# Retention heads: squares kept as a high and a low part, summed by two matmuls in the middle of the next unit

## The chip, the cores and the metric

One core of one Trainium2 chip runs one program. The metric is the device time of one execution in microseconds (us); lower is better. The engines are TensorE (PE), VectorE (DVE), ScalarE (ACT), GpSimd (POOL) and the DMA queues. Each engine works through its own list of instructions in order, and engines meet only at semaphores.

## The reference

Two transformer blocks follow each other on 512 tokens of width 1024. The change touches the retention branch of the second block's mixer: 8 heads, keys of 64, values of 128. Cut to what matters:

```python
def _retention(q, k, v, gn_gain):
    inner = jnp.einsum('bhncd,bhnkd->bhnck', qc, kc) * decay
    ...
    o = (o_inner + o_cross).reshape(B, H, S, dv)
    mu = jnp.mean(o, axis=-1, keepdims=True)
    var = jnp.mean(jnp.square(o - mu), axis=-1, keepdims=True)
    on = (o - mu) * lax.rsqrt(var + GN_EPS) * gn_gain
    return on...

r_out = jax.nn.silu(g_r) * _retention(...)
gate_a, gate_r = jnp.split(jax.nn.sigmoid(g_merge), 2, axis=-1)
mixed = gate_a * (a_out @ w_branch_nsa) + gate_r * (r_out @ w_branch_ret)
```

Everything is kept transposed: the 128 features of a head lie on the partitions and the 512 tokens along the row. So the variance of a token is a sum over partitions, which the kernel takes as a matmul with a 128x128 matrix of ones. The values are centred beforehand, so `o - mu` is what the value matmuls give.

## The kernel before

Nearly all products are done in three matmuls (`mm3`, lines 177 to 179): an operand is split into a high part that the fast type (fp32r) holds, made by ACT as a copy, and a low part, the difference, made by DVE or POOL; then high by high, high by low and low by high are added in one PSUM bank. A sum of squares is done otherwise: one matmul on plain fp32 data, `ones` by `gn_sq`.

Weights come in chunks of 128x1024 from DRAM into two raw buffers `w_raw`. ACT makes `w_hi` (line 146), DVE makes `w_lo` (line 151), and when that is done SP issues the load of the chunk after next (line 2652). Conversion runs two chunks ahead of PE.

The retention stage has 8 units, one for each head `h`. It follows the attention of the same mixer, and its queue orders are written out by hand. In unit `h`:

- PE (`pe_part`, line 2329): `score(h+1)`, then `squares_summed(h-1)` (line 2346), then the first four tiles of `fill(h)` (a 1024-wide product that makes one tile of the merge gates, 24 matmuls in all), `values(h)` (12 matmuls), then the other four tiles of `fill(h)`. After unit 7 comes `squares_summed(7)`, and then the merge's first two products with the attention output (`pair_by_parts`, line 2503: 32 matmuls on `a_hi`, 16 on `a_lo`), the same with `r_hi` and `r_lo`, and the other chunks of the merge.
- DVE (line 2439): `weigh(h+1)` (scores by decay, `weighted`), `w_lo` of a chunk, then `normalise(h-1)`: reciprocal of `gn_r`, `r_raw` by it (line 2458), `r_raw` by `gr_silu` (line 2462).
- ACT (line 2370): in units 2 and 4 loads and high parts for the next pair of heads, then `ws_hi` of `h+1` (line 2375), `w_hi` of a chunk, the root `gn_r` of `h-1` (line 2381), the copy `r_raw` of `h` out of PSUM (line 2416), `gn_sq` of `h` (line 2418), in units 5 to 7 some tiles of `a_hi`, then `gm_out` of `h` (line 2430) and its store.
- POOL (line 2481): in units 0, 2, 4 `rq_lo` and `rk_lo` (line 2300), the load of a decay table, `ws_lo` of `h+1` (line 2485), in units 5 to 7 some tiles of `a_lo` (line 2498). After the stage it issues the loads of the gates for the merge (line 2607), and ACT, when `r_hi` is complete, the load of the residual `x` (2 MB).

There is one `gn_sq` buffer, one `gn_r` buffer and one PSUM bank (5) for the sum; `var` counts the sums done, `root` the roots.

Of the kernel before, what the change touches and what calls it, by code (L numbers as in the profile page):

```python
# [79 lines left out]
def build_program(nc, stream, xt, cols, tables, rows, decays, pos, w2, out):  # L80
    top = ExitStack()
    with top:
# [1389 lines left out]
        ws_lo = sb("ws_lo", [P, OFF[TB]], F32R, A0 + 5 * K)  # L1472
        gn_sq = sb("gn_sq", [P, S], F32, A0 + 12 * K)
        gn_r = sb("gn_r", [P, S], F32, A0 + 10 * K)

        rv_t = sb("rv_t", [P, S], F32, 40 * K)
        rv_hi_out = sb("rv_hi_out", [P, S], F32R, 42 * K)
# [320 lines left out]
        def sparse_attention(start):  # L1798
# [26 lines left out]
            first_act, first_pool, first_pe, retain = retention(s)  # L1825

            def pe_part(pe):
                pe.wait_ge(s["zero"], 1)
                pe.wait_ge(q["out"], 12)

                def score(U):
# [170 lines left out]

            def centring(dve):
                nc.vector.tensor_scalar(centre[:], ident[:], 1.0 / P, None, ALU.subtract).then_inc(s["zero"], 1)

            def act_part(act):

# [266 lines left out]
        def retention(nsa):  # L2274
# [5 lines left out]
            y0 = merges["y"]  # L2280
            fgm, fm = FIRST["b2_gm"], FIRST["b2_merge"]
            HEADS = 8
            R_FIRST = range(3)
            nsa_outs = atts["out"]
            A_TILES = {5: range(0, 3), 6: range(3, 6), 7: range(6, 8)}
# [43 lines left out]
            def pe_part(pe):  # L2329
                def values(h):  # L2330
                    at_least(pe, s["square"], h - 1)
                    pe.wait_ge(rv_in[h // 2 % 2], 32 * (h // 4 + 1))
                    for n, kb in enumerate(ORDER_K):
                        pe.wait_ge(s["lo"], 4 * h + n + 1)
                        w, at = slice(kb * P, (kb + 1) * P), slice(KOFF[kb], KOFF[kb + 1])
                        mm3(banks[6 + h % 2][:, kb * P:S], rv_hi[:, h // 2 % 2, h % 2, w], rv_lo[:, h // 2 % 2, h % 2, w],
                            ws_hi[:, at], ws_lo[:, at], n == 0, n == TB - 1).then_inc(s["summed"], 1)

                def fill(h, slot, tiles):
                    for k in tiles:  # L2340
                        w = slice(k * P, (k + 1) * P)
                        last = mm3(banks[3 + h % 2][:], w_hi[:, slot, w], w_lo[:, slot, w], xn_hi[:, k, :], xn_lo[:, k, :],
                                   k == 0, k == KT - 1)
                    return last

                def squares_summed(h):
                    pe.wait_ge(s["square"], h + 1)
                    at_least(pe, s["root"], h)
                    nc.tensor.matmul(banks[5][:], ones[:], gn_sq[:], start=True, stop=True).then_inc(s["var"], 1)

                for h in range(HEADS):
                    if 0 < h < HEADS - 1:
                        score(pe, h + 1)
                    if h:
                        squares_summed(h - 1)
                    slot = ready(pe, fgm, h)
                    if h == 0:
                        pe.wait_ge(nsa["cleared"], 32)
                    at_least(pe, s["cleared"], h - 1)
                    fill(h, slot, range(0, 4))  # L2360
                    if h:
                        values(h)
                    fill(h, slot, range(4, KT)).then_inc(used, 1)
                    if h == 0:
                        score(pe, 1)
                        pe.wait_ge(nsa["out"], 16 + nsa_outs)
                        values(0)
                squares_summed(HEADS - 1)

            def act_part(act):  # L2370
# [32 lines left out]
                for h in range(HEADS):  # L2403
# [12 lines left out]
                    nc.scalar.activation(r_raw[:, h, :], banks[6 + h % 2][:], ACT.Copy).then_inc(s["out"], 1)  # L2416
                    at_least(act, s["var"], h)
                    nc.scalar.activation(gn_sq[:], banks[6 + h % 2][:], ACT.Square).then_inc(s["square"], 1)
                    for k in A_TILES.get(h, ()):
                        act.wait_ge(s["staged_lo"], 8)  # L2420
                        act.wait_ge(nsa["out"], 16 + nsa_outs)
                        nc.scalar.activation(a_hi[:, k, :], a_raw[:, k, :], ACT.Copy).then_inc(y["y_hi"], 1)
# [58 lines left out]
            def pool_part(pool):  # L2481
                def lows(h):
                    for n, kb in enumerate(ORDER_K):
                        pool.wait_ge(s["hi"], 4 * h + n + 1)
                        nc.gpsimd.tensor_tensor(ws_lo[:, KOFF[kb]:KOFF[kb + 1]], weighted[:, KOFF[kb]:KOFF[kb + 1]],
                                                ws_hi[:, KOFF[kb]:KOFF[kb + 1]], ALU.subtract).then_inc(s["lo"], 1)

                lows(0)
                for h in range(HEADS):
                    if h % 2 == 0 and h < 6:  # L2490
                        low_qk(pool, h // 2 + 1)
                    if h + 2 < HEADS:
                        decay_to(pool, h + 2)
                    if h + 1 < HEADS:
                        lows(h + 1)
                    for k in A_TILES.get(h, ()):
                        pool.wait_ge(y["y_hi"], y0 + k + 1)
                        nc.gpsimd.tensor_tensor(a_lo[:, k, :], a_raw[:, k, :], a_hi[:, k, :],
                                                ALU.subtract).then_inc(y["y_lo"], 1)
# [341 lines left out]
```

## Time and profile before

| what | value |
|---|---|
| median of 3 runs | 2182.56 us (2181.18 to 2183.87) |
| the profiled execution, its time | 2178.03 us |
| the span in its profile | 2176.2 us |
| around the span | 1.8 us |
| granted TensorE clock | 0.99 of full on average, 1.00 in the retention stage |
| retention stage, from `values(0)` to the last sum | about 1590 to 1666 us of the span |

The page gives busy time for each engine, the busy share in 40 slices, and the chain that ended last. For a change of a few instructions inside one stage these totals say little; the stage itself is read in the timeline of each engine, where each row is one instruction or a run of like ones, with the idle time before it and who ended that in brackets.

### The profile page before, as it was taken

How to read it: one execution, taken by the hardware profiler on the slowest of the kernel's cores; microseconds unless marked ns; L12 is line 12 of the kernel's file. 1: busy time of each engine (PE TensorE's matmuls, PEld its weight loads, DVE VectorE, ACT ScalarE, POOL GpSimd, SP SyncE). 2: the span in 40 equal slices, each digit the busy share in tenths (PEclk: the TensorE clock that was granted, in tenths of full speed). 3: DMA queues.
4: the chain of work that ended last, by engine and by line, in shares of the span. 5: the costliest groups of instructions: out<-in, count | busy, mean ns of one | idle time of the engine just before them, and what ended most of it. 6: DMA issues, size and time to landing. Idle time of an engine off the chain costs nothing.

```text
span 2176.2 us, 28422 instructions
## 1 busy us (share of the span) xinstructions
PE 2126.0 (98%) x9960; PEld 1758.9 (81%) x9960; DVE 1183.0 (54%) x1981; ACT 896.9 (41%) x1542; POOL 467.0 (21%) x359
## 2 busy tenths in 40 slices
PE   8999999999999999999998999999999999999997
PEld 6788888888878888887886788888877888888786
DVE  5466764544442264443277777788767435444324
ACT  4355664422221242222133467676645424222212
POOL 2012344211110042210015601111165313111000
PEclk9999999999999999999999999999999999999999
DMA  4212244323333323333324322222264432233331
GB/s 169 78 54 73 83 151 154 95 91 96 97 104 97 97 82 97 95 96 106 97 97 144 118 68 69 83 73 76 87 215 171 139 97 88 96 97 96 109 97 64
DMA packets 66505, 222.91 MB, mean 102 GB/s; under 512 B 7312, under 2 KB 7568, under 8 KB 66032
## 3 DMA queue, kind: packets, MB, share of 16 engines
q1 hardware_dynamic: 51120, 182.08, 27.2%
q10 hardware_dynamic: 11712, 27.27, 3.4%
q0 software_dynamic: 3584, 12.39, 1.6%
q8 instruction: 54, 0.88, 0.2%
q14 instruction: 35, 0.29, 0.0%
HBM read 202.31 MB, written 18.87 MB: 102 GB/s over the span
## 4 chain that ended last, share of the span: by engine, by line
PE 82%; DVE 8%; ACT 3%; DMA 3%; POOL 3%; issue 2%; DVEq 0%; SPq 0%; ACTq 0%; POOLq 0%
PE bank L177 24%; PE bank L179 24%; PE bank L178 24%; PE bank L183 3%; PE bank L184 3%; DMA w_raw<-stream 2%; POOL hid L540 2%; PE bank L1848 2%; DVE w_lo L151 2%; DVE gn_r L2454 1%; ACT w_hi L146 1%; PE bank L676 1%; DVE xn_lo L455 1%; DMA m_more<-spill_g 1%; POOL hid L1235 1%
## 5 line engine op out<-in xcount | busy, mean ns | idle before, releaser
L151 DVE TENSOR_TENSOR w_lo<-w_raw,w_hi 128x1024 fp32r<-128x1024 f32 x337 | 464.3, 1381 | 539.3 <-ACT w_hi L146 538.7
L177 PE MATMUL bank<-xn_hi,w_hi 128*128 128x512 f32 x1624 | 647.6, 399 | 9.2 <-DVE w_lo L151 5.9
L179 PE MATMUL bank<-xn_hi,w_lo 128*128 128x512 f32 x1624 | 634.4, 391 | 0.0
L178 PE MATMUL bank<-xn_lo,w_hi 128*128 128x512 f32 x1624 | 633.7, 390 | 0.0
L146 ACT ACTIVATE w_hi<-w_raw 128x1024 fp32r<-128x1024 f32 x337 | 353.9, 1053 | 390.9 <-PE bank L179 242.8
L177 PEld LDWEIGHTS bank<-xn_hi,w_hi 128*128 128x128 f32 x1624 | 306.1, 189 | 73.0 <-DVE w_lo L151 7.4
L179 PEld LDWEIGHTS bank<-xn_hi,w_lo 128*128 128x128 f32 x1624 | 305.4, 188 | 64.7
L178 PEld LDWEIGHTS bank<-xn_lo,w_hi 128*128 128x128 f32 x1624 | 306.1, 188 | 62.8 <-issue 2.6
L177 PE MATMUL bank<-h_hi,w_hi 128*128 (+1 forms) x528 | 205.9, 390 | 4.1 <-DVE hid L476 3.7
L546 POOL TENSOR_TENSOR h_lo<-hid,h_hi 128x512 f32 (+1 forms) x66 | 85.6, 1296 | 564.7 <-ACT h_hi L406 564.7
L178 PE MATMUL bank<-h_lo,w_hi 128*128 (+1 forms) x528 | 205.5, 389 | 0.0
L179 PE MATMUL bank<-h_hi,w_lo 128*128 (+1 forms) x528 | 205.4, 389 | 0.0
L406 ACT ACTIVATE h_hi<-hid 128x512 f32 (+1 forms) x66 | 41.8, 634 | 290.2 <-DVE hid L476 290.2
L177 PEld LDWEIGHTS bank<-h_hi,w_hi 128*128 128x128 f32 x528 | 99.1, 188 | 26.7 <-DVE hid L476 5.3
L178 PEld LDWEIGHTS bank<-h_lo,w_hi 128*128 128x128 f32 x528 | 99.1, 188 | 20.6
L179 PEld LDWEIGHTS bank<-h_hi,w_lo 128*128 128x128 f32 x528 | 99.1, 188 | 20.5
L402 ACT ACTIVATE silu<-silu 128x512 f32<-128x512 f32 x66 | 41.7, 632 | 174.4 <-DVE silu L466 174.4
L472 DVE TENSOR_TENSOR hid<-bank,norm_r 128x512 f32<-128x512 f32 x66 | 45.6, 690 | 111.9 <-PE bank L179 111.9
L2040 ACT ACTIVATE npt_hi<-bank 128x512 fp32r<-128x512 f32 (+3 forms) x128 | 48.7, 432 | 69.3 <-PE bank L1848 69.2
L2159 DVE TENSOR_TENSOR npt_lo<-bank,npt_hi 128x512 fp32r<-128x512 f32 (+3 forms) x128 | 56.7, 485 | 35.1 <-ACT npt_hi L2040 35.1
L2032 ACT ACTIVATE nprob<-nprob,small 128x128 f32<-128x128 f32 (+3 forms) x128 | 71.1, 558 | 9.9 <-DVE small L2135 9.4
L466 DVE TENSOR_TENSOR silu<-bank,norm_r 128x512 f32<-128x512 f32 x66 | 45.6, 691 | 45.2 <-PE bank L179 45.0
(414 smaller groups left out, 3118.2 us busy)
## 6 DMA issues: line engine op xcount, KB each, us to landing
w_raw<-stream SPq DMA_DIRECT2D x337, 512.0 KB, 3.6
spill_g<-gate_out ACTq DMA_DIRECT2D x16, 256.0 KB, 2.0
m_more<-spill_g POOLq DMA_DIRECT2D x3, 1024.0 KB, 13.4
x<-xt SPq DMA_DIRECT2D x4, 512.0 KB, 6.8
x<-xt ACTq DMA_DIRECT2D x1, 2048.0 KB, 10.3
spill_x<-x ACTq DMA_DIRECT2D x1, 2048.0 KB, 6.3
spill_ga<-ga_out ACTq DMA_DIRECT2D x8, 256.0 KB, 2.0
spill_rv_hi<-rv_hi_out ACTq DMA_DIRECT2D x8, 256.0 KB, 2.4
```

Of the source, the lines that this page charges most:

```text
L146: nc.scalar.activation(w_hi[:, slot, :], w_raw[:, slot % 2, :], ACT.Copy).then_inc(split_hi, 1)
L151: nc.vector.tensor_tensor(w_lo[:, slot, :], w_raw[:, slot % 2, :], w_hi[:, slot, :], ALU.subtract).then_inc(split_lo, 1)
L177: nc.tensor.matmul(to, a_hi, b_hi, start=start, stop=False, skip_group_check=True)
L178: nc.tensor.matmul(to, a_hi, b_lo, start=False, stop=False, skip_group_check=True)
L179: return nc.tensor.matmul(to, a_lo, b_hi, start=False, stop=stop, skip_group_check=True)
L183: nc.tensor.matmul(to, both, first, start=start, stop=False, skip_group_check=True)
L184: return nc.tensor.matmul(to, both, second, start=False, stop=stop, skip_group_check=True)
L466: nc.vector.tensor_tensor(silu[:, t, :], banks[bank][:], norm_r[:], ALU.mult).then_inc(s["scaled"], 1)
L546: nc.gpsimd.tensor_tensor(h_lo[:, bass.ds(i * 2 * S + t * S, S)], hid[:, t, :], h_hi[:, bass.ds(i * 2 * S + t * S, S)], ALU.subtract).then ...
L2032: nc.scalar.activation(at, at, ACT.Exp, bias=neg_top[:, n:n + 1], scale=0.125, accum_out=total[:, n:n + 1]).then_inc(s["exp"], 1)
L2040: nc.scalar.activation(npt_hi[:, KOFF[kb]:KOFF[kb + 1]], banks[4 + kb % 2][:, 0:S - kb * P], ACT.Copy).then_inc(s["hi"], 1)
L2159: nc.vector.tensor_tensor(npt_lo[:, at], banks[4 + kb % 2][:, 0:S - kb * P], npt_hi[:, at], ALU.subtract).then_inc(s["lo"], 1)
```

## The change

Five edits:

- ACT writes a new tile `gn_hi`, a copy of `gn_sq` in fp32r, right behind `gn_sq`, after a wait for `gn_sq` itself.
- POOL writes `gn_lo`, `gn_sq` minus `gn_hi`, behind `ws_lo` of `h+1` and ahead of the `a_lo` tiles.
- `squares_summed` becomes two matmuls on fp32r data, `ones_r` by `gn_hi` and `ones_r` by `gn_lo`, with a wait for the one part and for the other.
- In PE's list `squares_summed(h-1)` stands no longer ahead of the first half of `fill(h)` but behind it, ahead of `values(h)`.
- DVE makes `ones_r` once, far ahead of the stage, behind `centre`; PE waits for it at the start of the attention part.

```diff
+        gn_hi = sb("gn_hi", [P, S], F32R, A0 + 14 * K)
+        gn_lo = sb("gn_lo", [P, S], F32R, A0 + 60 * K)
+        ones_r = sb("ones_r", [P, P], F32R, 98 * K + 512)
...
-                pe.wait_ge(s["zero"], 1)
+                pe.wait_ge(s["zero"], 2)
...
                 nc.vector.tensor_scalar(centre[:], ident[:], 1.0 / P, None, ALU.subtract).then_inc(s["zero"], 1)
+                nc.vector.tensor_copy(ones_r[:], ones[:]).then_inc(s["zero"], 1)
...
+            g, g0 = norm_sems, count_up(hi=HEADS, low=HEADS)
...
                 def squares_summed(h):
-                    pe.wait_ge(s["square"], h + 1)
+                    pe.wait_ge(g["hi"], g0["hi"] + h + 1)
                     at_least(pe, s["root"], h)
-                    nc.tensor.matmul(banks[5][:], ones[:], gn_sq[:], start=True, stop=True).then_inc(s["var"], 1)
+                    nc.tensor.matmul(banks[5][:], ones_r[:], gn_hi[:], start=True, stop=False)
+                    pe.wait_ge(g["low"], g0["low"] + h + 1)
+                    nc.tensor.matmul(banks[5][:], ones_r[:], gn_lo[:], start=False, stop=True).then_inc(s["var"], 1)
 
                 for h in range(HEADS):
                     if 0 < h < HEADS - 1:
                         score(pe, h + 1)
-                    if h:
-                        squares_summed(h - 1)
                     slot = ready(pe, fgm, h)
                     if h == 0:
                         pe.wait_ge(nsa["cleared"], 32)
                     at_least(pe, s["cleared"], h - 1)
                     fill(h, slot, range(0, 4))
                     if h:
+                        squares_summed(h - 1)
                         values(h)
                     fill(h, slot, range(4, KT)).then_inc(used, 1)
...
                     nc.scalar.activation(gn_sq[:], banks[6 + h % 2][:], ACT.Square).then_inc(s["square"], 1)
+                    act.wait_ge(s["square"], h + 1)
+                    nc.scalar.activation(gn_hi[:], gn_sq[:], ACT.Copy).then_inc(g["hi"], 1)
...
                     if h + 1 < HEADS:
                         lows(h + 1)
+                    pool.wait_ge(g["hi"], g0["hi"] + h + 1)
+                    nc.gpsimd.tensor_tensor(gn_lo[:], gn_sq[:], gn_hi[:], ALU.subtract).then_inc(g["low"], 1)
```

PE in unit 6, before: the sum for head 5 stands between the last score products (`rq`, `rk`) and the fill (`xn`, `w`).

```order
L177 MATMUL bank<-rq_hi,rk_hi 128x256
L178 MATMUL bank<-rq_lo,rk_hi 128x256
L179 MATMUL bank<-rq_hi,rk_lo 128x256
L2349 MATMUL bank<-gn_sq,ones 128x512
L177 MATMUL bank<-xn_hi,w_hi 128x512
```

The same engine and unit after the change: the two matmuls stand between the first half of the fill and the value products (`ws`, `rv`).

```order
L177 MATMUL bank<-xn_hi,w_hi 128x512
L178 MATMUL bank<-xn_lo,w_hi 128x512
L179 MATMUL bank<-xn_hi,w_lo 128x512
L2354 MATMUL bank<-gn_hi,ones_r 128x512
L2356 MATMUL bank<-gn_lo,ones_r 128x512
L177 MATMUL bank<-ws_hi,rv_hi 128x512
```

The sum has moved 12 matmuls down the list; in unit 7, which has no scores, likewise.

ACT in unit 7, before: root of head 6, copy and square of head 7, then the `a_hi`, `r_hi` and `gm_out` tiles.

```order
L2381 ACTIVATE gn_r<-bank,col 128x512
L2416 ACTIVATE r_raw<-bank 128x512
L2418 ACTIVATE gn_sq<-bank 128x512
L2422 ACTIVATE a_hi<-a_raw 128x512 x2
L2395 ACTIVATE r_hi<-r_raw 128x512 x3
L2430 ACTIVATE gm_out<-bank 128x512
```

The same place on ACT after the change:

```order
L2387 ACTIVATE gn_r<-bank,col 128x512
L2422 ACTIVATE r_raw<-bank 128x512
L2424 ACTIVATE gn_sq<-bank 128x512
L2426 ACTIVATE gn_hi<-gn_sq 128x512
L2430 ACTIVATE a_hi<-a_raw 128x512 x2
L2401 ACTIVATE r_hi<-r_raw 128x512 x3
L2438 ACTIVATE gm_out<-bank 128x512
```

One activation more stands ahead of `a_hi`, `r_hi` and `gm_out`, as it does ahead of `gm_out` in every unit.

POOL in units 6 and 7, before: the four `ws_lo` pieces of head 7, then the `a_lo` tiles of units 6 and 7 in a row, then the loads of the merge gates.

```order
L2485 TENSOR_TENSOR ws_lo<-weighted,ws_hi 128x512
L2485 TENSOR_TENSOR ws_lo<-weighted,ws_hi 128x384
L2485 TENSOR_TENSOR ws_lo<-weighted,ws_hi 128x128
L2485 TENSOR_TENSOR ws_lo<-weighted,ws_hi 128x256
L2498 TENSOR_TENSOR a_lo<-a_raw,a_hi 128x512 x5
L2607 DMA m_temps<-spill_ga 128x2x512
```

The same place on POOL after the change:

```order
L2493 TENSOR_TENSOR ws_lo<-weighted,ws_hi 128x128
L2493 TENSOR_TENSOR ws_lo<-weighted,ws_hi 128x256
L2505 TENSOR_TENSOR gn_lo<-gn_sq,gn_hi 128x512
L2508 TENSOR_TENSOR a_lo<-a_raw,a_hi 128x512 x3
L2505 TENSOR_TENSOR gn_lo<-gn_sq,gn_hi 128x512
L2508 TENSOR_TENSOR a_lo<-a_raw,a_hi 128x512 x2
L2617 DMA m_temps<-spill_ga 128x2x512
```

A subtraction stands ahead of the three `a_lo` tiles of unit 6 and another ahead of the two of unit 7.

## Rows read from the trace of the kernel before

**Rows 1.** The page, busy time of each engine over the whole span

```profile
PE 2126.0 (98%) x9960; PEld 1758.9 (81%) x9960; DVE 1183.0 (54%) x1981; ACT 896.9 (41%) x1542; POOL 467.0 (21%) x359
```

**Rows 2.** What PE waited for, 1560 to 1700 us: total, times, longest

```profile
PE bank L177 <- POOL rk_lo L2300: 1.2, 1, 1.2
PE bank L177 <- DVE w_lo L151: 1.2, 1, 1.2
PE bank L2349 <- ACT gn_sq L2418: 0.3, 1, 0.3
```

**Rows 3.** Timeline of PE, units 2 and 6: start, duration, instruction

```profile
1605.91 1.12 PE L2349 MATMUL bank<-gn_sq,ones 128*128 128x512 f32 x2
...
1607.11 0.40 PE L178 MATMUL bank<-xn_lo,w_hi 128*128 128x512 f32 x1
1607.34 0.39 PE L179 MATMUL bank<-xn_hi,w_lo 128*128 128x512 f32 x1
...
1648.17 1.12 PE L2349 MATMUL bank<-gn_sq,ones 128*128 128x512 f32 x2
```

**Rows 4.** Timeline of PE, end of unit 7

```profile
1665.37 1.02 PE L2349 MATMUL bank<-gn_sq,ones 128*128 128x512 f32 x2
...
1666.46 0.40 PE L2515 MATMUL bank<-a_hi,w_lo 128*128 128x512 f32 x1
```

**Rows 5.** Timeline of DVE, units 4 and 6 and the end of the stage

```profile
1631.52 1.67 DVE L2449 TENSOR_TENSOR weighted<-bank,decay 128x512 f32<-128x512 f32 x4
...
1652.01 1.67 DVE L2449 TENSOR_TENSOR weighted<-bank,decay 128x512 f32<-128x512 f32 x4
...
1662.55 1.21 DVE L151 TENSOR_TENSOR w_lo<-w_raw,w_hi 128x1024 fp32r<-128x1024 f32 x1
1663.69 3.34 DVE L2454 RECIPROCAL gn_r<-gn_r 128x512 f32<-128x512 f32 x1
1667.06 0.75 DVE L2458 SCALAR_TENSOR_TENSOR r_raw<-r_raw,col,gn_r 128x512 f32<-128x512 f32 x1
...
1675.18 2.35 DVE L151 TENSOR_TENSOR w_lo<-w_raw,w_hi 128x1024 fp32r<-128x1024 f32 x2
```

**Rows 6.** Timeline of ACT, unit 7

```profile
1661.02 0.69 ACT L2381 ACTIVATE gn_r<-bank,col 128x512 f32<-128x512 f32 x1 [0.51 <-DVE r_raw L2458]
1662.82 0.60 ACT L2416 ACTIVATE r_raw<-bank 128x512 f32<-128x512 f32 x1 [1.11 <-PE bank L179]
1663.32 0.59 ACT L2418 ACTIVATE gn_sq<-bank 128x512 f32<-128x512 f32 x1
1663.79 0.63 ACT L2422 ACTIVATE a_hi<-a_raw 128x512 fp32r<-128x512 f32 x1
```

**Rows 7.** Timeline of POOL, subtractions in units 0, 2, 6 and 7

```profile
1593.73 3.35 POOL L2485 TENSOR_TENSOR ws_lo<-weighted,ws_hi 128x512 fp32r<-128x512 f32 x4
...
1608.56 1.37 POOL L2300 TENSOR_TENSOR rq_lo<-r_qk,rq_hi 128x512 fp32r<-128x512 f32 x1 [3.45 <-ACT rq_hi L2294]
...
1657.83 4.25 POOL L2498 TENSOR_TENSOR a_lo<-a_raw,a_hi 128x512 fp32r<-128x512 f32 x3
1664.50 2.54 POOL L2498 TENSOR_TENSOR a_lo<-a_raw,a_hi 128x512 fp32r<-128x512 f32 x2 [2.42 <-ACT a_hi L2422]
```

**Rows 8.** The chain that ended last, from the last split of the stage to PE

```profile
1676.57 10.30 DMA w_raw<-stream
...
1689.36 0.47 PE bank L177
```

**Rows 9.** DVE against POOL: DVE rows of units 0 to 2

```profile
1593.54 4.63 DVE L151 TENSOR_TENSOR w_lo<-w_raw,w_hi 128x1024 fp32r<-128x1024 f32 x1 [2.90 <-ACT w_hi L146]
...
1608.87 1.60 DVE L2462 TENSOR_TENSOR r_raw<-r_raw,gr_silu 128x512 f32<-128x512 f32 x1
...
1619.74 0.69 DVE L2462 TENSOR_TENSOR r_raw<-r_raw,gr_silu 128x512 f32<-128x512 f32 x1
```

**Rows 10.** Timeline of DVE, where the new copy of the ones goes

```profile
1201.66 0.97 DVE L2004 TENSOR_SCALAR centre<-ident 128x128 f32<-128x128 f32 x1
```

## The prediction

> **What bounds the kernel now.** I read the page first: PE is busy 98% of the span [rows 1], so by its totals anything taken from PE is gain. Then the stage: in 1560 to 1700 us PE has three waits by name, 1.2 us for a low part that POOL makes, 0.3 us for the last-but-one `gn_sq`, and 1.2 us for a `w_lo` [rows 2]. The first is over before the change sets in. The last decides: the chain that ended last runs, at the end of the stage, not over PE but over DVE and a DMA. DVE splits two chunks in a row from 1675.18 on, SP then issues the load of a `w_raw` at 1676.57, which lands after 10.30 us (a residual of 2 MB and the gates are loaded at the same time), and PE goes on at 1689.36 [rows 5, 8], after the 1.2 us of idle [rows 2]. So PE is already early there, and time taken from PE in the stage is lost at that point unless DVE's work or the load also moves.
>
> How much room has DVE? PE needs (1648.17 - 1605.91) / 4 = 10.57 us for a unit [rows 3]. DVE starts `weighted` at 1631.52 and two units later at 1652.01 [rows 5], 10.25 us for a unit, and catches up only where nothing holds it. DVE's loop is 0.3 us for a unit shorter than PE's, not more. And at the end DVE is the longer one: from 1662.55 to 1677.5 its instructions follow one another [rows 5].
>
> **PE's sum.** The fp32 matmul starts at 1605.91; the second matmul of the fill behind it starts at 1607.11, and matmuls follow each other at 1607.34 - 1607.11 = 0.23 us. So the fill began at 1606.88 and the sum cost 0.97 us. At the end of the stage: 1666.46 - 0.23 - 1665.37 = 0.86 us [rows 3, 4]. The two new ones have the shape of their neighbours: 2 x 0.23 = 0.46 us. Saved are 0.40 to 0.51 us a head, 8 heads 3.2 to 4.1 us, and the wait of 0.3 us goes, since the sum now comes 12 matmuls = 2.7 us later. The change of row layout behind the scores stays, in front of the fill. PE's own sum: -3.5 to -4.4 us, which would be the whole effect if nothing else bound.
>
> Going down 2.7 us the list, `var` comes later for ACT, but in its list the root stands behind `ws_hi` of the next head, which waits for `values(h)`, and these stand behind the sum anyway. This costs nothing in units 1 to 6. `gn_sq` has one buffer, and its rewriting waits for `var`; it too stands behind `values(h)`. Nothing.
>
> **ACT's and POOL's additions.** `gn_hi` is one ACT copy of 128x512: 0.63 us as `a_hi` takes [rows 6], plus a few hundredths for the wait for `gn_sq`, 8 times. In units 0 to 6 ACT waits afterwards for `weighted` or for PE, so it is covered; what it pushes are `gm_out` (needed one unit later) and in units 2 and 4 `rq_hi`. If that cover were gone, it were 8 x 0.7 = 5.4 us. `gn_lo` is one POOL subtraction, 1.29 us by 1.37 for `rq_lo` and 4.25 / 3 for `a_lo` [rows 7], say 1.3. PE needs it 0.23 us after `gn_hi`. Only once does PE wait for `gn_sq` at the old place [rows 2]; else it is done by then. The chain `gn_hi`, `gn_lo` takes 0.7 + 1.35 = 2.05 us, and the new place is 2.7 + 0.2 us later. It just fits, as long as PE is not early by more than the rest.
>
> Unit 1 is the tight one. The old sum of head 0 stands one unit ahead of 1605.91 [rows 3], at 1595.3; the new one at 1595.3 + 2.7 = 1598.0. POOL runs four `ws_lo` pieces from 1593.73 to 1597.08 [rows 7], and DVE's `w_lo`, begun at 1593.54, took 4.63 us instead of 1.21 [rows 9, 5]: it got through only when POOL paused. With `gn_lo` behind the four pieces either DVE waits until 1598.4 and the next `weighted` begins 0.5 us later, or POOL waits and PE stands until 1599.4, 1.1 us, and `values(1)`, on which `ws_hi` waits, start 0.4 us later. Taken: +0.5 us on DVE's loop, bounds 0 and +1.3.
>
> **Where the two engines collide.** A DVE instruction with two inputs in SBUF is stretched when POOL subtracts: line 2462 took 1.60 us beside `rq_lo` and 0.69 alone [rows 9, 7]. The Trainium skill ("SBUF — State Buffer", "SBUF: two separate sides") says that the port pair is an exclusive lock for the whole instruction, taken by whoever starts first. By it, eight more subtractions could be eight blocks of up to 1.3 us each on DVE.
> The rows place them thus: from a root's start ACT takes 0.6 to `r_raw`, 0.50 to `gn_sq`, 0.6 for it and 0.7 for `gn_hi` [rows 6], so `gn_lo` runs from 2.4 to 3.7 us after; DVE is then in the reciprocal, from 0.7 to 4.0 us after, 3.34 us with one input [rows 5]. Taken: no block in units 1 to 6. In units 2 and 4 `rq_lo` comes 0.7 us later than now and misses line 2462: 1.60 - 0.69 = 0.9 us back at one place, at the other 0 to 0.9.
> At the end it goes the other way. `a_lo` of unit 6 (1657.83 to 1662.08) ends 1.3 us later and lies over the `w_lo` of 1662.55: up to +0.8. `a_lo` of unit 7 (1664.50) moves behind `gn_lo` to about 1665.5 to 1668.2 and lies over lines 2458 and 2462 of head 6, the first at 1667.06: 0 to +1.3 [rows 5, 7].
> DVE's sum at 1675.18: +0.5 (0 to +1.3) for unit 1; -0.9 to -1.8 for `rq_lo`; 0 to +2.1 at the end; and where `ws_hi` waits for PE's `values`, which come earlier, 0 to -0.6 (the room of two units, 0.3 us each). Ends: -2.4 and +2.5. I take the middle, 0.
>
> **The last sum.** Here the new chain shows. Root of head 6 at 1661.02 waits for DVE (0.51 us), so `r_raw` of head 7 can start at 1661.6 at best and not 3.8 us early; `gn_sq` starts 0.50 later [rows 6] and ends at 1662.7, `gn_hi` at 1663.4, `gn_lo` at 1664.8, the sum at 1665.0. Now it ends at 1666.23. PE would be there at 1661.5 and waits over 3 us. Of PE's 3.5 to 4.4 us 1.2 are left, plus or minus DVE's shift. `gm_out` of head 7 comes about 1 us earlier (1.11 us of ACT's wait for PE less 0.7 for `gn_hi` [rows 6]), and with it POOL's gate loads, which then compete a little less with the `w_raw` of 1676.57: 0 to -1.2 us, taken -0.4.
>
> **The ones.** `ones_r` is one more DVE copy behind `centre` (0.97 us [rows 10], a 128x128 tile): 0.2 to 1.0 us before a `w_lo`. PE could stand for 0 to 0.7 us there, with later waits of its own before the stage to take it up. Taken 0.
>
> **Sum.** PE resumes at 1689.36 + 0 (DVE) - 0.4 (load) = -0.4 us; behind it PE runs without a wait in what is left of the stage's view, so the end moves by as much. Profiled execution: 2178.03 - 0.4 = 2177.6. The median of the runs shown is 4.5 us above that execution, so 2182.56 - 0.4 = **2182.2 us**. Own bounds: -2.4 - 1.2 = -3.6, where PE's 1.2 us idle plus 1.2 us allow no more than about -2.5, to +2.5 + 0.7 for the ones: 2180.1 to 2185.8.
>
> **Rivals.**
> (a) PE's gain arrives whole. For it: PE 98% busy [rows 1]. Against: 1.2 us of idle behind a DMA [rows 2, 8]. It needs DVE 3 to 4 us earlier, more than the 0.3 us a unit and every collision gone. -3.5 to -4.4: about 2178.6.
> (b) The lock decides, slower. Place: DVE in every unit. If `gn_lo` starts just ahead of lines 2458, 2462 or `w_lo`, DVE loses 0.9 to 1.3 us a unit, its loop becomes 10.25 + 1.1 = 11.35 us, over PE's new 10.1 and old 10.57. Over 8 units 8 x 1.1 = 8.8, less the 0.3 us a unit of room, 2.4: +6.4, about 2189. It decides once the block is over 0.3 us a unit. For it: line 2462's 0.9 us and `w_lo`'s 4.63 [rows 9]. Against it: the reciprocal covers 3.34 us [rows 5]. The exclusive lock of the Trainium skill ("SBUF — State Buffer", "Who interferes with whom") would make it so, and those two rows agree with it.
> (c) Only the end collides, and unit 1: +1 to +2.5 us, about 2184.3. Same mechanism, two places.
> (d) The change is not what it says: the fp32r sum with `ones_r` costs as much as the old one. Then PE wins nothing, DVE's sum is the same: 2182 to 2184.
>
> **Chances.** Forecast 0.66; (a) 0.08; (b) 0.05; (c) 0.18; (d) 0.03. 0.2% is 4.4 us, about what a measurement of this kernel can tell from no change. (a) reaches it in half its cases: faster 0.04. (b) nearly always: slower 0.05. Within 0.2%: 0.91. The range takes in forecast, (c) and half of (a), with the 1.3 us by which the runs differ from their median: 2178.8 to 2186.0.
>
> **What would show it.** New sums of 0.46 us on PE, and a wait of over 2 us for `gn_lo` in front of the last sum. A wait for it in unit 1. DVE's two splits at 1675 within 1.5 us of before, and PE's wait for `w_lo` behind the first merge chunks grown from 1.2 us to 2 or more. It is wrong if PE has no such wait there (a), if `weighted` of successive units are over 10.6 us apart (b), or if the `w_raw` load lands in well under or over 10 us, which I have only from one execution.

## The result: 0.17% slower, and where the profile shows it

| | median of 12 runs | lowest to highest |
|---|---|---|
| before | 2182.4 us | 2180.5 to 2185.78 |
| after | 2185.27 us | 2183.87 to 2189.75 |

The ratio is 1.0017, with a 95% interval of 1.0009 to 1.0024: slower by 2 to 5 us, clear of no change. The profiled execution of after took 2185.58 us, its span 2183.6 us. Ratios here and below are of fast executions alone; left out as slow is one of moved_load_first_early, at 10305 us.

The page's first group, engine and busy time, answers to [rows 1]:

```profile
PE 2128.3 (97%) x9960; PEld 1761.6 (81%) x9960; DVE 1191.7 (55%) x1982; ACT 900.0 (41%) x1550; POOL 473.9 (22%) x367
```

The waits of PE by name from 1565 to 1700 us (engine, instruction, what it waited for: us in total, times, longest) answer to [rows 2]:

```profile
PE bank L2356 <- POOL gn_lo L2505: 3.8, 4, 1.5
PE bank L177 <- POOL rk_lo L2305: 1.2, 1, 1.2
PE bank L177 <- DVE w_lo L151: 0.7, 1, 0.7
PE bank L2523 <- issue: 0.6, 1, 0.6
PE bank L2354 <- ACT gn_hi L2426: 0.4, 1, 0.4
```

PE now waits 4.2 us for the two parts, as much as the shorter sums were to save. The five waits are in units 4, 5 and 7 and ahead of the last sum. The sums themselves are short. Timeline of PE in unit 2 (start, duration, line, operation), to set beside [rows 3]:

```profile
1613.60 0.39 PE L2354 MATMUL bank<-gn_hi,ones_r 128*128 128x512 f32 x1
1613.83 0.39 PE L2356 MATMUL bank<-gn_lo,ones_r 128*128 128x512 f32 x1
1614.05 0.39 PE L177 MATMUL bank<-ws_hi,rv_hi 128*128 128x512 f32 x1
```

They start 0.23 us apart and the next product 0.22 us later: 0.45 us, for the 0.97 us of before. A unit in which PE does not wait got 0.40 us shorter: the same matmul of unit 3 starts 1623.77 - 1613.60 = 10.17 us later, where before needed 10.57 [rows 3].

```profile
1623.77 0.39 PE L2354 MATMUL bank<-gn_hi,ones_r 128*128 128x512 f32 x1
```

What went wrong stands on DVE. Its timeline after, units 0 to 3, and then the end of the stage; this answers to [rows 5, 9]:

```profile
1598.69 5.90 DVE L151 TENSOR_TENSOR w_lo<-w_raw,w_hi 128x1024 fp32r<-128x1024 f32 x1 [2.89 <-ACT w_hi L146]
...
1614.00 0.69 DVE L2470 TENSOR_TENSOR r_raw<-r_raw,gr_silu 128x512 f32<-128x512 f32 x1
1614.61 1.68 DVE L2457 TENSOR_TENSOR weighted<-bank,decay 128x512 f32<-128x512 f32 x4
1617.87 5.47 DVE L151 TENSOR_TENSOR w_lo<-w_raw,w_hi 128x1024 fp32r<-128x1024 f32 x1 [1.57 <-ACT w_hi L146]
...
1628.10 1.68 DVE L2457 TENSOR_TENSOR weighted<-bank,decay 128x512 f32<-128x512 f32 x4
...
1669.40 2.32 DVE L151 TENSOR_TENSOR w_lo<-w_raw,w_hi 128x1024 fp32r<-128x1024 f32 x1
...
1675.02 0.87 DVE L2466 SCALAR_TENSOR_TENSOR r_raw<-r_raw,col,gn_r 128x512 f32<-128x512 f32 x1
...
1683.61 2.35 DVE L151 TENSOR_TENSOR w_lo<-w_raw,w_hi 128x1024 fp32r<-128x1024 f32 x2
```

The same place of unit 2 before, DVE's timeline:

```profile
1610.39 1.67 DVE L2449 TENSOR_TENSOR weighted<-bank,decay 128x512 f32<-128x512 f32 x4
1613.65 1.94 DVE L151 TENSOR_TENSOR w_lo<-w_raw,w_hi 128x1024 fp32r<-128x1024 f32 x1 [1.58 <-ACT w_hi L146]
...
1620.35 1.68 DVE L2449 TENSOR_TENSOR weighted<-bank,decay 128x512 f32<-128x512 f32 x4
```

`w_lo` of unit 2 took 1.94 us and takes 5.47. From one `weighted` to the next it was 1620.35 - 1610.39 = 9.96 us and is 1628.10 - 1614.61 = 13.49, 3.5 us more. What POOL did at that time, before:

```profile
1611.56 0.56 POOL L2308 DMA_DIRECT2D decay<-decays  x1
1612.14 4.46 POOL L2485 TENSOR_TENSOR ws_lo<-weighted,ws_hi 128x512 fp32r<-128x512 f32 x4
```

and after, answering to [rows 7]:

```profile
1617.05 0.56 POOL L2313 DMA_DIRECT2D decay<-decays  x1
1617.63 3.37 POOL L2493 TENSOR_TENSOR ws_lo<-weighted,ws_hi 128x512 fp32r<-128x512 f32 x4
1620.96 1.28 POOL L2505 TENSOR_TENSOR gn_lo<-gn_sq,gn_hi 128x512 fp32r<-128x512 f32 x1
1622.19 0.56 POOL L2313 DMA_DIRECT2D decay<-decays  x1
```

Before, `w_lo` started 1.51 us into POOL's run, got in after the second subtraction, and the four took 4.46 us with DVE's 1.1 in their middle. After, it starts 0.24 us into the run and gets in only when all four and `gn_lo` are through: the run takes 3.37 + 1.28 us without a break, and `w_lo` ends (1623.34) 1.1 us behind it. Why it starts earlier in the run: the two steps that I had counted on. `gn_hi` stands in front of `rq_hi` on ACT, so `rq_lo`, `rk_lo`, the load and the run come 0.7 us later; and since `rq_lo` then misses line 2470 (0.69 us, where it was 1.60), DVE comes 0.9 us sooner. That makes 1.6 us; the rows give 1.51 - 0.24 = 1.27.

The chain at the stage's end, answering to [rows 8], is still a load. DVE's first late split is at 1683.61, 88.5 us after the first `rq_hi` of the stage (1595.12), and was at 1675.18, 85.2 us after it (1589.97): 3.3 us later.

```profile
1685.00 9.31 DMA w_raw<-stream
```

PE goes on at 1696.79, 101.7 us after `rq_hi`, where it was 1689.36, 99.4: 2.3 us later. The other 5.15 us between the two profiles are in front of the stage. They can't be put down to the change: in the twelve profiles below of kernels with `ones_r`, `rq_hi` starts between 1591.3 and 1597.7, and in the four without it between 1592.0 and 1597.3. The two profiles differ there in the clock: ahead of the stage the granted clock stands at 0.50 for 24 us in before and for 38 us in after, and half of the difference, 7 us, is what PE could lose by it. In the stage it is 1.00 in both.

PE itself is late too, before it gets to that load. Timeline of PE at the end of unit 7, to set beside [rows 4]:

```profile
1672.91 0.50 PE L2356 MATMUL bank<-gn_lo,ones_r 128*128 128x512 f32 x1 [1.49 <-POOL gn_lo L2505]
...
1673.47 0.40 PE L2525 MATMUL bank<-a_hi,w_lo 128*128 128x512 f32 x1
```

The merge's second product starts 78.4 us after the first `rq_hi`, and in before 76.5: PE has lost 1.9 us inside the stage. So DVE's delay reaches PE in two ways: through `weighted`, `ws_lo` and `gn_lo`, for which PE waits in the stage, and through the load behind the late splits.

### The profile page after: what moved, and what is told of

Its sections match the earlier page's. It is cut to its first block, busy times and chain, and to the rows that moved or that the text cites. A ratio compares the mean times of both kernels' runs of the same rounds, so it can differ in the third digit from the quotient of the medians.

```text
span 2183.6 us, 28439 instructions
## 1 busy us (share of the span) xinstructions
PE 2128.3 (97%) x9960; PEld 1761.6 (81%) x9960; DVE 1191.7 (55%) x1982; ACT 900.0 (41%) x1550; POOL 473.9 (22%) x367
## 4 chain that ended last, share of the span: by engine, by line
PE 81%; DVE 8%; ACT 3%; DMA 3%; POOL 2%; issue 2%; DVEq 0%; SPq 0%; ACTq 0%; POOLq 0%
PE bank L177 24%; PE bank L179 24%; PE bank L178 24%; PE bank L184 3%; PE bank L183 3%; DMA w_raw<-stream 2%; POOL hid L540 2%; DVE w_lo L151 2%; PE bank L1851 2%; DVE gn_r L2462 1%; ACT w_hi L146 1%; DVE xn_lo L455 1%; PE bank L676 1%; DMA m_more<-spill_g 1%; POOL hid L1235 1%
## 5 line engine op out<-in xcount | busy, mean ns | idle before, releaser
L151 DVE TENSOR_TENSOR w_lo<-w_raw,w_hi 128x1024 fp32r<-128x1024 f32 x337 | 471.5, 1403 | 539.4 <-ACT w_hi L146 538.9
```

The source lines that it names most:

```text
L151: nc.vector.tensor_tensor(w_lo[:, slot, :], w_raw[:, slot % 2, :], w_hi[:, slot, :], ALU.subtract).then_inc(split_lo, 1)
```

## Experiments

Each time is the median, the ratio is to before on the same chip, with its 95% interval. The columns behind it are from one profile each: `w_lo` of units 0 and 2; the first of the two late splits, counted from the stage's first `rq_hi`; and PE's wait for a `w_lo` in the merge.

| kernel | us | ratio | `w_lo` 0 | `w_lo` 2 | late split | PE waits |
|---|---|---|---|---|---|---|
| before | 2182.4 | 1 | 4.63 | 1.94 | 85.2 | 1.2 |
| after | 2185.27 | 1.0017 [1.0009, 1.0024] | 5.90 | 5.47 | 88.5 | 0.7 |
| ones_only | 2181.82 | 0.9991 [0.9982, 1.0] | 4.62 | 2.97 | 87.5 | 3.4 |
| moved_fp32 | 2183.0 | 0.9999 [0.999, 1.0008] | 4.65 | 2.97 | 85.5 | 2.7 |
| parts_unused | 2186.39 | 1.0015 [1.0006, 1.0024] | 5.88 | 5.03 | 89.6 | 3.6 |
| split_old_place | 2192.78 | 1.0038 [1.0023, 1.0052] | 5.83 | 2.70 | 93.5 | 1.9 |
| hi_only | 2184.07 | 1.0011 [1.0002, 1.002] | 4.64 | 3.80 | 88.3 | 2.1 |
| lo_only | 2185.16 | 1.002 [1.0011, 1.0029] | 5.63 | 1.95 | 87.5 | 0.9 |
| after_early_split | 2182.17 | 1.0007 [0.9998, 1.0016] | 5.89 | 5.46 | 83.7 | none |
| load_between | 2187.81 | 1.0032 [1.002, 1.0044] | 1.98 | 1.56 | 89.8 | 0.7 |
| after_load_first | 2181.51 | 0.9995 [0.9985, 1.0004] | 2.00 | 1.54 | 85.3 | 2.3 |
| before_load_first | 2181.85 | 0.9999 [0.9989, 1.0009] | 2.01 | 1.53 | 85.3 | 1.9 |
| after_first_u0 | 2185.04 | 1.0018 [1.0008, 1.0028] | 1.98 | 5.41 | 89.7 | 3.2 |
| after_first_u2 | 2181.43 | 1.0004 [0.9993, 1.0014] | 5.89 | 1.58 | 84.9 | 2.4 |
| lo_only_first | 2186.36 | 1.0019 [1.0007, 1.003] | 2.00 | 1.53 | 87.5 | 2.4 |
| after_load_first_early | 2178.83 | 0.9983 [0.9974, 0.9991] | 2.00 | 1.54 | 80.4 | none |
| before_load_first_early | 2180.72 | 0.9991 [0.9982, 1.0] | 2.00 | 1.53 | 82.1 | none |
| moved_load_first_early | 2178.6 | 0.9985 [0.9976, 0.9994] | 1.99 | 1.53 | 80.6 | none |

One profile scatters too: ones_only has the stage of before, yet its `w_lo` of unit 2 takes 2.97 us and its late split is 2.3 us later. Most of the 2.3 is the granted clock: from 5.6 to 9.1 us after the first `rq_hi` it is 0.50 (the lower level, 1.2 GHz), matmuls start 0.43 us apart and not 0.23, and PE loses 1.7 us. The profiles of hi_only, load_between, before_load_first_early and after_first_u0 have the same stretch, that of split_old_place one twice as long, and that of parts_unused one in unit 4. PE's place and the late split of these seven are later by up to that much; before, after and the other nine have 1.00 up to the late splits. The 2.97 us are not the clock: moved_fp32 has them too at 1.00. There, as in before, `w_lo` starts 1.51 us into POOL's run, so before's 1.94 us is the luckier of two outcomes. So verdicts here go by the medians, and the profiles say which instruction waits for which.

### One part of the change at a time

The ones alone (`ones_r` behind `centre`, PE waits for it, the rest as before):

```diff
+                nc.vector.tensor_copy(ones_r[:], ones[:]).then_inc(s["zero"], 1)
```

> The kernel before with the ones_r copy on DVE and PE's wait for it, nothing else. Stage time below means: from the start of the first rq_hi of unit 0 on ACT to the first a_hi matmul behind the wait for w_lo in the merge; it was 99.4 us before (1589.97 to 1689.36) and 101.7 us after (1595.12 to 1696.79). If the slowdown comes from the retention stage: time within 0.05% of before, stage 99.4, and the wait of PE for w_lo near 1230 us as before (0.65 us). If the copy of the ones shifts DVE against POOL upstream (the rival): +1 to +3 us, and that wait is near 1.9 us as it was after the change.

The place alone, one fp32 matmul, no parts:

```diff
-                    if h:
-                        squares_summed(h - 1)
                     slot = ready(pe, fgm, h)
...
                     if h:
+                        squares_summed(h - 1)
                         values(h)
```

> The kernel before with only the move: the one fp32 sum stands behind the first half of the fill. Lock theory: nothing is added to ACT or POOL, so DVE runs as before; PE loses its 0.3 us wait and gains nothing at the merge; stage 99.2 to 99.5, time -0.2 to +0.1 us. Rival, that the later sum delays the roots: DVE's last two splits (1675.18) come 1 us or more later, time +1 us or more.

The parts made and not used: ACT and POOL as in the change, PE sums `gn_sq` in fp32 at the old place, ACT waits for `gn_lo` before it rewrites `gn_sq`:

```diff
-                    nc.tensor.matmul(banks[5][:], ones_r[:], gn_hi[:], start=True, stop=False)
-                    pe.wait_ge(g["low"], g0["low"] + h + 1)
-                    nc.tensor.matmul(banks[5][:], ones_r[:], gn_lo[:], start=False, stop=True).then_inc(s["var"], 1)
+                    nc.tensor.matmul(banks[5][:], ones[:], gn_sq[:], start=True, stop=True).then_inc(s["var"], 1)
```

> gn_hi and gn_lo are made by ACT and POOL as after the change, but PE sums gn_sq in fp32 at its old place, so the parts go unused (ACT waits for gn_lo before it rewrites gn_sq). Lock theory: the slowdown is all here: w_lo of unit 0 near 5.9 us, w_lo of unit 2 over 5 us, DVE's last two splits 3 us later than before relative to the stage's start, stage 101.5 to 102.5, time +2 to +3.5 us. Rival, that the two matmuls and their place are the cause: stage 99.4 to 99.9, time within 0.5 us of before.

Parts and two matmuls, but at the old place, in front of the fill:

```diff
+                    if h:
+                        squares_summed(h - 1)
                     slot = ready(pe, fgm, h)
...
                     if h:
-                        squares_summed(h - 1)
                         values(h)
```

> The change without the move: two fp32r sums where the one stood. PE waits there for gn_lo, at least 1.5 us in units 1 and 7. Lock theory: DVE's pattern decides, stage 101.5 to 103. If PE's waits decide: they add 1 to 2 us in most units, stage over 105.

Measured: 0.9991, 0.9999, 1.0015 and 1.0038. Neither the ones nor the place costs anything; making the parts costs by itself as much as the whole change (1.0017). And the new place makes the two matmuls bearable. At the old one PE waits for `gn_lo` in unit 1, PE's timeline of split_old_place:

```profile
1606.10 0.79 PE L2356 MATMUL bank<-gn_lo,ones_r 128*128 128x512 f32 x1 [2.50 <-POOL gn_lo L2506]
```

In all it waits there 5.3 us for `gn_lo` and 1.3 for `gn_hi`. Its 1.0038 is not all waits: the mean granted clock of its four runs is 0.987, and 0.990 in before. How much each is worth isn't separated.

Then the parts apart. hi_only leaves `gn_lo` out, and `gn_hi` is not used. lo_only leaves `gn_hi` out: POOL subtracts `gn_sq` from itself, and the result is not used. Both sum in fp32 at the old place.

```diff
+                    pool.wait_ge(s["square"], h + 1)
+                    nc.gpsimd.tensor_tensor(gn_lo[:], gn_sq[:], gn_sq[:], ALU.subtract).then_inc(g["low"], 1)
```

> Of the parts only gn_hi is made, on ACT, and nobody uses it; PE sums gn_sq in fp32 at its old place. DVE end below means the start of the first of the two w_lo at the end of the stage, from the stage's start: 85.2 before, 88.5 after the change, 89.6 with both parts made. Theory A, the half microsecond that gn_hi puts ahead of rq_hi moves POOL's run of ws_lo over w_lo of unit 2: that w_lo takes 4 us or more (the run without gn_lo), w_lo of unit 0 stays at 4.6, the last units are as before; DVE end 86.5 to 88, time +1 to +2.5 us. Theory B, only POOL's extra work hurts: w_lo of unit 2 under 3 us, DVE end and time as before.

> Of the parts only a subtraction of the size of gn_lo is made, on POOL (gn_sq less itself, which keeps its length and leaves the parts out of the computation; nobody uses it); PE sums gn_sq in fp32 at its old place. Theory A: w_lo of unit 0 near 5.9 us, w_lo of unit 2 under 3 us, the w_lo of unit 7 near 2.3 us instead of 1.2; DVE end 86 to 87.5, time +0.5 to +1.5 us, so that the two halves add up to the whole. Theory B: as with both parts, DVE end over 88 and time +2.5 us or more.

Measured: 1.0011 and 1.002. `gn_hi` alone, which nothing reads, makes `w_lo` of unit 2 3.80 us long: it now starts 0.68 us into the run, where it starts at 1.50 in ones_only, with the same stretch of low clock. In parts_unused it starts at 0.67 as well, and `gn_lo` lengthens the run and the wait by 1.2: 5.03 us. lo_only is as slow as the change without a long `w_lo` in unit 2, which stayed open until lo_only_first, below.

### The late splits

In the merge, ACT and DVE treat its first two chunks behind the last root and the last `normalise`. after_early_split puts them ahead (ACT likewise):

```diff
+                for j in range(2):
+                    ahead(low_part, dve, fm, j)
                 normalise(HEADS - 1)
-                for j in range(2):
-                    ahead(low_part, dve, fm, j)
```

> The changed kernel, with ACT's and DVE's work on the two merge chunks put ahead of the last head's root and normalisation at the end of the stage. If DVE's late splits and the load behind them carry the slowdown to PE: the w_raw load is issued 4 us or more earlier, PE's wait for w_lo in the merge goes, and the time falls by 2 to 4 us against the changed kernel, to -1 to +1 us against before. If something else sets the time: no change, +2.5 us against before.

Measured: 1.0007, so some 2 of the change's 3 to 4 us come back although `w_lo` of unit 2 is as long as it was (5.46), and PE has no wait in the merge. So the load behind the late splits does hold PE up. But it is not the whole path of the loss. The same edit gives the kernels without the long wait as much: 0.9999 to 0.9991 and 0.9995 to 0.9983 (the last section of experiments). And the change still stands 0.16% above before_load_first_early (0.9991), since PE comes to the merge as late as in after: its second product starts 78.4 us after the first `rq_hi` in both, and 75.1 us in after_load_first, where the waits for `gn_lo` are 1.7 us and not 3.8.

### Where the load stands

The long waits of `w_lo` were all in runs that follow the issue of a decay load. load_between puts that load between `ws_lo` and `gn_lo`:

```diff
-                    if h + 2 < HEADS:
-                        decay_to(pool, h + 2)
                     if h + 1 < HEADS:
                         lows(h + 1)
+                    if h + 2 < HEADS:
+                        decay_to(pool, h + 2)
```

> The changed kernel, with POOL's issue of the decay load moved from ahead of the four ws_lo pieces to between them and gn_lo. If DVE gets the port at any gap in POOL's run: w_lo of unit 0 near 4.6 us and of unit 2 near 4.2 us or less, DVE end 1 to 2.5 us earlier than with the change, time +0 to +2 us against before. If it gets in only where POOL waits for a semaphore: 5.9 and 5 us stay or only one of them changes, since the run of unit 2 starts 0.6 us earlier against w_lo.

`w_lo` of units 0 and 2 fell to 1.98 and 1.56, yet the kernel is not faster: 1.0032, from six runs, where I expected 0 to +2 us. The wait has moved to where the load now is. Timelines of POOL and DVE in unit 5 of load_between:

```profile
1651.22 0.56 POOL L2313 DMA_DIRECT2D decay<-decays  x1
1651.80 1.31 POOL L2505 TENSOR_TENSOR gn_lo<-gn_sq,gn_hi 128x512 fp32r<-128x512 f32 x1
1653.05 3.78 POOL L2508 TENSOR_TENSOR a_lo<-a_raw,a_hi 128x512 fp32r<-128x512 f32 x3
```

```profile
1653.57 3.83 DVE L2466 SCALAR_TENSOR_TENSOR r_raw<-r_raw,col,gn_r 128x512 f32<-128x512 f32 x1
```

Line 2466 takes 0.75 us alone and 3.83 here, until the run of four is over. The run, not the tile or the instruction, is what matters, and the load ahead of it.

after_load_first and before_load_first issue the decay load ahead of `rq_lo` and `rk_lo`, so that in units 0, 2 and 4 the `ws_lo` run has two subtractions and no load in front of it, in the change and in before:

```diff
+                    if h + 2 < HEADS:
+                        decay_to(pool, h + 2)
                     if h % 2 == 0 and h < 6:
                         low_qk(pool, h // 2 + 1)
-                    if h + 2 < HEADS:
-                        decay_to(pool, h + 2)
```

> The changed kernel, with POOL's issue of the decay load ahead of rq_lo and rk_lo instead of directly ahead of the ws_lo run. Load theory: a DVE instruction waits past one POOL instruction only in a run that follows such an issue directly; so w_lo of unit 0 falls from 5.9 to at most 2.5 us and that of unit 2 from 5.5 to at most 2.5, DVE end from 88.5 to 84 to 86, time 2 to 3.5 us under the changed kernel, 0 to +1 us against before (the end's collisions stay, 1.1 us). Rival, that the length of the run or the phase decides: 5 us and more stay in unit 2, time +2.5 us.

> The kernel before with the same move of the load. Load theory: w_lo of unit 0 falls from 4.6 to at most 2.5 us, but weighted of unit 1 then waits for the decay load or starts up to 1.5 us earlier; PE is the longer loop for the rest, DVE end 84 to 85.2; time -1 to 0 us. Rival: 4.6 stays, no change.

Measured: 0.9995 and 0.9999. The change's loss is gone, and before gains nothing, although its `w_lo` of unit 0 falls from 4.63 to 2.01: DVE has 2.6 us of room there.

Is it unit 2 alone? after_first_u0 has the new order in unit 0 only, after_first_u2 in unit 2 only:

```diff
+                    if h == 2:
+                        decay_to(pool, h + 2)
                     if h % 2 == 0 and h < 6:
                         low_qk(pool, h // 2 + 1)
-                    if h + 2 < HEADS:
+                    if h + 2 < HEADS and h != 2:
```

> The change, with the decay load put ahead of rq_lo and rk_lo in unit 0 only. Theory (one run of subtractions behind a load decides, that of unit 2): w_lo of unit 0 falls from 5.90 to about 2.0 us, yet weigh of unit 2 starts where it did (20.6 to 20.7 us after the stage's start, as in the kernels with all three loads first), the w_lo of unit 2 stays at 5.0 to 5.5 us, and the ratio to before stays at 1.0015 to 1.002. Rival (what counts is unit 0, the one both lo_only and the change have longer): ratio 0.9995 to 1.0005. Rival (each part of the load order gives a share): about 1.0007.

> The change, with the decay load put ahead of rq_lo and rk_lo in unit 2 only. Theory: w_lo of unit 0 stays 5.9 us, that of unit 2 falls from 5.47 to 1.5 us, weigh of unit 3 starts 3.5 to 3.9 us earlier, DVE's first of the two late splits comes 85 to 86 us after the stage's start and not 88.5, and the ratio to before is 0.9995 (0.999 to 1.0002). Rival (unit 0 counts): ratio stays 1.0015 to 1.002.

Measured: 1.0018 and 1.0004. Unit 0's wait of 5.90 us can stay or go; unit 2's is the 0.2%. The two medians, measured side by side, lie 3.6 us apart, but their intervals overlap. What carries the verdict with them is after_load_first, whose interval lies wholly below that of after. In after_first_u2, timelines of POOL and DVE in unit 2, and DVE's in unit 0:

```profile
1612.03 1.29 POOL L2305 TENSOR_TENSOR rk_lo<-r_qk,rk_hi 128x512 fp32r<-128x512 f32 x1
1613.28 4.37 POOL L2493 TENSOR_TENSOR ws_lo<-weighted,ws_hi 128x512 fp32r<-128x512 f32 x4
1617.61 1.29 POOL L2507 TENSOR_TENSOR gn_lo<-gn_sq,gn_hi 128x512 fp32r<-128x512 f32 x1
```

```profile
1594.91 5.89 DVE L151 TENSOR_TENSOR w_lo<-w_raw,w_hi 128x1024 fp32r<-128x1024 f32 x1 [2.89 <-ACT w_hi L146]
...
1614.09 1.58 DVE L151 TENSOR_TENSOR w_lo<-w_raw,w_hi 128x1024 fp32r<-128x1024 f32 x1 [1.58 <-ACT w_hi L146]
```

The same subtractions follow one another as closely as in after, `w_lo` starts 0.81 us into `ws_lo`, and it is through after 1.58 us: it waited for no more than the instruction in progress. POOL paid 1.0 us for it (4.37, where undisturbed runs take 3.37).

### What the lone subtraction costs

lo_only_first is lo_only with the loads first:

> POOL's subtraction alone (gn_sq minus gn_sq, unused, sum in fp32 at the old place), with the decay loads ahead of rq_lo and rk_lo. lo_only was 1.002 of before although its trace shows no long w_lo in unit 2. Theory (its 0.2% was such a run too, in unit 0 or in executions that the trace does not show): 0.999 to 1.0005, w_lo of units 0 and 2 at 2.0 and 1.5 us. Rival (POOL's eight subtractions cost by themselves, by plain collisions or by holding back gn_sq for the next head): 1.0015 to 1.0025, as lo_only was.

Measured: 1.0019, with no long `w_lo` left. So the rival held: lo_only's 0.2% does not come from the load. DVE's timeline in unit 5 of lo_only_first shows another place, and the POOL rows beside it:

```profile
1653.75 1.75 DVE L2466 SCALAR_TENSOR_TENSOR r_raw<-r_raw,col,gn_r 128x512 f32<-128x512 f32 x1
```

```profile
1651.42 1.05 POOL L2505 TENSOR_TENSOR gn_lo<-gn_sq 128x512 fp32r<-128x512 f32 x1
1652.41 4.24 POOL L2508 TENSOR_TENSOR a_lo<-a_raw,a_hi 128x512 fp32r<-128x512 f32 x3
```

`a_lo` comes 1.0 us later, and its pieces now start just ahead of line 2466: 1.75 us, not 0.75, with `weighted` of the next unit 1.0 us later and the late split 2.2 us later than in before_load_first. That is an ordinary collision of one instruction. That it makes the 0.2% is read from this one profile; no run takes it away. The change does not have it (its line 2466 takes 0.75 to 0.78 us in units 1 to 6), since there PE's moved sum lets the whole stage run ahead of it; that last link is argued from the rows, not tried.

### Does the change pay once both are mended?

after_load_first_early, before_load_first_early and moved_load_first_early hold the loads first and the splits early, for the change, for before, and for before with only the sum moved.

> The changed kernel with both mends, the load first and the merge's two chunks converted ahead of the last normalisation. If PE's saving of 3.2 to 4.4 us was only hidden behind DVE's chain: PE's waits for gn_lo but the last are gone, no wait in the merge, time -2 to -5 us against before, the first version that is faster. If the last sum's chain (gn_sq, gn_hi, gn_lo) is the new bound: -0.5 to -2 us.

> The kernel before with both mends. No wait of PE in the merge (1.2 us), nothing taken off PE: time -1 to -1.5 us. If this is as fast as the changed kernel with both mends, the split into parts is worth nothing here even with its harm removed; if the parts pay, that one is 1 to 3 us faster than this.

> Before, with the fp32 sum moved behind the first half of the fill, the loads first, and the merge's first two splits ahead of the last root and normalise; no parts. The change with the same two mends was 0.9983, before with them 0.9991. Theory (with the cover mended the two fast matmuls pay what they save on PE): this one is as before with the mends, 0.9988 to 0.9993. Rival (the move is what pays): 0.9981 to 0.9985, as the change with the mends.

Measured: 0.9983, 0.9991 and 0.9985. With both edits the change is 0.17% faster than before. Against before with the same two edits, measured side by side, its median is 1.9 us lower, though the intervals overlap. But moving the sum alone, in fp32 and without `gn_hi`, `gn_lo` and `ones_r`, does the same: my expectation that the fast matmuls pay was not met, and the two are too near each other to tell apart. A good part of what PE saves on the sums it waits for their parts: its second product of the merge starts 75.1 us after the first `rq_hi`, and 76.1 us in moved_load_first_early. Waits of PE in the stage, after_load_first_early:

```profile
PE bank L2356 <- POOL gn_lo L2505: 1.7, 2, 1.5
```

In moved_load_first_early PE has no wait in the stage but that of 1.2 us for `rk_lo` that all kernels share. The late splits are at 80.4 and 80.6 us. The simpler kernel is the one I would keep.

## The prediction, point by point

Forecast were 2182.2 us, 0.4 less than before; measured are 2185.27, 2.9 more. The time lies in the range (2178.8 to 2186.0) and within 0.2% of before, but on the other side of it. That it lies in the range is luck: the range reached so far up by the end of the stage, the ones and scatter, and not by the block in unit 2.

- **PE's sum**: right for the sum, 0.45 us for 0.97 and 0.86. The unit got shorter by 0.40 us, the low end of the 0.40 to 0.51 forecast.
- **What bounds**: right in part. The late splits and their load do hold PE up: in after_load_first PE reaches the merge 1.4 us earlier than in before, waits 2.3 us for `w_lo` there and is no faster. But I had PE arriving early, with a wait of 2 us or more at that load. It arrives 1.9 us late and waits 0.7. "It just fits", for the chain `gn_hi`, `gn_lo`, holds only while DVE is on time.
- **`gn_hi` and `gn_lo` by themselves**: right in size (`gn_lo` 1.28 us), covered on ACT.
- **Unit 1**: I took +0.5 on DVE and a wait of PE for `gn_lo`. `w_lo` of unit 0 is 1.3 us longer and the next `weighted` begins 0.4 later. PE does not wait there. after_first_u0 shows that it costs nothing.
- **`rq_lo`**: right. 0.9 us back at one place, none at the other; this is also what leads to the loss.
- **The step that failed** is "Taken: no block in units 1 to 6", and with it DVE's sum of 0 with ends of -2.4 and +2.5. I had looked at which subtractions are added and where `gn_lo` would lie, and had found the reciprocal there. I had not looked at what the 0.7 us do to the run of `ws_lo` that was already there, against a `w_lo` that was already there. That block is +3.5 us (+2.5 against the 2.97 us that `w_lo` takes in moved_fp32); with -0.9 ahead of it, -0.9 in units 3 to 6 and +1.6 at the end, DVE's sum is +3.3, outside my ends.
- **The end**: 0 to +2.1 forecast, +1.6 measured: 1.1 on `w_lo` at 1669.40 (I allowed 0.8), the rest on line 2466 and a wait of 0.46 behind it.
- **The last sum**: forecast a wait of over 3 us for `gn_lo`; it is 1.5, and 2.7 us of waits for the parts come earlier, in units 4, 5 and 7, because DVE's delay reaches PE there first.
- **The load**: forecast -0.4; 9.31 us for 10.30. In the other kernels with late splits PE goes on 13.2 to 16.1 us after the first one, in before 14.2: scatter, and no effect can be read.
- **The ones**: right, 0.9991.
- **Rival (b)** was the mechanism, priced as one instruction a unit in every unit. It was a whole run, once. Its sign that `weighted` comes over 10.6 us apart appears in one unit (13.49). I gave it 0.05 and its row [rows 9] held the hint: `w_lo` of 4.63 us is 3.4 us of waiting, which is not one subtraction (3.35 / 4 = 0.8 us, [rows 7]) but the whole run of four. The edits that take the block away, after_load_first and after_first_u2, bring the time back to before.

## What to carry to other kernels

When an edit shifts an instruction by half a microsecond, look at what long-standing neighbour it slides under, not only at where the new instructions lie: here an added copy on ACT was free on ACT and cost 3.5 us on DVE, two engines on. On GpSimd, do not issue a load directly ahead of a run of subtractions that VectorE's two-input work will meet; put it ahead of work that nobody meets. And a cheaper operation on the busiest engine pays only if its inputs come from engines with room at that moment: here, with the other two edits in place, moving one matmul did as much as the whole change.

## What the runs showed of the hardware

A DVE instruction with two inputs in SBUF that starts beside a POOL subtraction stays open until it gets in, so its duration shows the wait. From the stage's first `rq_hi` to 82 us after it, in all eighteen kernels' profiles, I compared each such duration with that of the same instruction alone and took waits of over 0.1 us. Where the POOL run had no DMA issue directly ahead, 191 of 191 waits were over at the end of the POOL instruction in progress, none longer than 1.1 us. Where an issue stood directly ahead, 20 of 29 went on past it, to the end of the run.

- 15 times DVE asked before the run was 0.7 us old, and all 15 waited for the whole run of 4 or 5 subtractions (2.6 to 4.7 us). In ten of them, all in unit 0, DVE's instruction starts 0.2 us ahead of the run's first subtraction, while POOL still issues the load [rows 7, 9]. Where no issue is directly ahead, DVE records that start 0.1 to 0.2 us before `rq_lo` are not held at all, and `rq_lo` takes 1.65 to 1.82 us, not 1.29.
- 13 times it asked 1.5 to 1.8 us into the run: 5 went to its end (1.5 to 3.1 us), 8 only past the one in progress (0.7 us). Without an issue ahead, 87 waits began 1.8 to 1.9 us into a run of 4 or more, and all 87 ended with the one in progress.
- The last was a run of one.

Moving the issue away ended the long wait each time, and load_between moved it along. No run has DVE ask in the first 1.7 us of a long run that no issue precedes; the nearest are 21 waits from the first 0.75 us of runs of two, and all ended with the first. So the engines of this kernel meet not only at semaphores, as the first section has it, but also here.

The Trainium skill ("SBUF — State Buffer", "SBUF: two separate sides") says that whoever starts first gets the shared pair for the whole instruction and the other blocks. The 191 agree; the 20 go beyond it, since there DVE was passed over at up to four boundaries between instructions, and in ten of them although its own record starts first. What in the issue of a load brings this about, no run here shows.
